# Seven more 1 MB weight buffers from spent storage, and more experts side by side in fours

## The reference, cut to what matters

```python
# first block: 32 experts, D_EXPERT = 256 (4 groups of 8: best group, then top 2 inside)
hid = silu(t @ w1[e]) * (t @ w3[e]);  out += gate[:, e] * (hid @ w2[e])
# second block: 16 experts, D_FF_EXPERT = 1024 (4 groups of 4: best group by its top-2 sum)
h = silu(t @ w_gate[e]) * (t @ w_up[e]);  y += gate[:, e] * (h @ w_down[e])
```

## Time and profile before

| what | us |
|---|---|
| median of 3 runs (lowest, highest) | 1676.85 (1676.71, 1677.9) |
| the profiled execution's own time | 1679.42 |
| its span, first to last instruction | 1676.2 |
| PE busy | 1570.4 (94%) |
| mean rate of DMA over the span | 241 GB/s, 404.40 MB |
| first mixture, first up matmul to last combine | about 727 to 962 |
| second mixture, the same | about 1189 to 1656 |

### The profile page before, as it was taken

The page is one execution under the profiler, slowest core; times in us unless marked ns, Lnnn a source line. Parts: engine busy times, 40 slices in busy tenths (PEclk is TensorE's granted clock), DMA queues, the critical chain, the costliest instruction groups (busy, mean ns, idle before and its releaser), DMA issues.

```text
span 1676.2 us, 21651 instructions
## 1 busy us (share of the span) xinstructions
PE 1570.4 (94%) x8351; PEld 1015.5 (61%) x8351; DVE 554.8 (33%) x1144; ACT 342.0 (20%) x731; POOL 148.8 (9%) x170
## 2 busy tenths in 40 slices
PE   6899999999999999999988999989999999999986
PEld 2577777677698888855544489658543544443433
DVE  2566767766522101262212110572501111101002
ACT  2344334344321100111100111441100000000001
POOL 1323442323200000000000000000000000000000
PEclk9999999999999999999999999999999999999999
DMA  9611111111944444549999974005499999999993
GB/s 374 252 39 46 42 44 43 38 38 50 373 151 136 145 151 151 199 169 389 421 421 421 421 268 151 25 1 181 194 422 421 421 408 421 421 422 400 422 421 140
DMA packets 58861, 404.40 MB, mean 241 GB/s; under 512 B 6766, under 2 KB 6898, under 8 KB 12576
## 3 DMA queue, kind: packets, MB, share of 16 engines
q1 hardware_dynamic: 52704, 381.92, 56.8%
q0 software_dynamic: 6080, 21.39, 4.3%
HBM read 402.19 MB, written 1.10 MB: 241 GB/s over the span
## 4 chain that ended last, share of the span: by engine, by line
PE 78%; DMA 9%; DVE 7%; issue 2%; ACT 2%; POOL 1%; SPq 1%; DVEq 0%; ACTq 0%; POOLq 0%
PE bank L656 76%; DMA ring<-in_moe 6%; DMA arena<-in_moe 2%; DVE arena L1728 2%; ACT arena L1370 1%; PE bank L1121 1%; POOL arena L600 1%; DMA xc<-in_xc 0%; DVE arena L1810 0%; ACT hc L1370 0%; DMA decay_rows<-arena 0%; DVE arena L1778 0%; DVE arena L1782 0%; DVE arena L1785 0%; DVE arena L1784 0%
## 5 line engine op out<-in xcount | busy, mean ns | idle before, releaser
L656 PE MATMUL bank<-arena 128*128 128x128 f32 (+3 forms) x3000 | 482.0, 311 | 28.6 <-DVE arena L1780 15.3
L656 PE MATMUL bank<-ring,arena 128*64 128x512 f32 (+2 forms) x1608 | 459.6, 604 | 25.3 <-DMA ring<-in_moe 18.1
L656 PEld LDWEIGHTS bank<-arena 128*128 128x128 f32 (+1 forms) x3000 | 394.3, 188 | 140.3 <-issue 50.3
L1370 ACT ACTIVATE arena<-bank 128x256 f32<-128x256 f32 (+2 forms) x372 | 161.2, 447 | 1112.7 <-PE bank L656 833.9
L656 PEld LDWEIGHTS bank<-ring,arena 128*64 128x64 f32 (+2 forms) x1608 | 144.1, 137 | 243.6 <-issue 239.1
L656 PE MATMUL bank<-hc,head_w 128*128 128x512 f32 (+1 forms) x384 | 162.5, 525 | 7.0 <-DVE arena L1802 6.6
L2130 DVE TENSOR_TENSOR arena<-arena,bank 128x256 f32<-128x256 f32 x48 | 20.2, 421 | 343.4 <-ACT arena L1370 343.4
L656 PE MATMUL bank<-arena,ring 128*128 128x256 f32 x416 | 92.3, 379 | 1.2 <-DVE arena L1907 1.2
L656 PE MATMUL bank<-hc,ring 128*128 128x256 f32 x416 | 91.4, 379 | 0.0
L656 PE MATMUL bank<-o_heads,arena 128*64 128x512 f32 (+2 forms) x184 | 85.3, 608 | 1.3 <-DMA ring<-in_moe 1.3
L656 PEld LDWEIGHTS bank<-arena,ring 128*128 128x128 f32 x416 | 79.0, 190 | 12.3 <-DVE arena L1907 1.6
(11 more groups left out here) (272 smaller groups left out, 1285.4 us busy)
## 6 DMA issues: line engine op xcount, KB each, us to landing
ring<-in_moe SPq DMA_DIRECT2D x201, 1024.0 KB, 17.3
ring<-in_dense SPq DMA_DIRECT2D x62, 1024.0 KB, 7.2
o_heads<-in_moe SPq DMA_DIRECT2D x23, 1024.0 KB, 18.1
xc<-in_moe SPq DMA_DIRECT2D x22, 1024.0 KB, 17.0
arena<-in_moe SPq DMA_DIRECT2D x21, 1024.0 KB, 19.4
hc<-in_moe SPq DMA_DIRECT2D x21, 1024.0 KB, 17.2
head_w<-in_head_w POOLq DMA_DIRECT2D x27, 512.0 KB, 3.9
xc<-in_dense SPq DMA_DIRECT2D x7, 1024.0 KB, 5.0
```

Of the source, the lines that this page charges most:

```text
L656: return nc.tensor.matmul(out, lhsT, rhs_, start=start, stop=stop, **kw)
L1370: return nc.scalar.activation(out, in_, func, **kw)
```

## The change

It turns seven more regions into homes for 1 MB loads. `ring` grows from 9 to 11, with storage from a smaller DMA scratch (`dynamic_dma_scratch_size=4096`) and from keeping the bias row of the spatial gating in the arena. Five spent regions join: `masks` (most of the constant matrices and ba_w, from load 37), `head_w` (from load 56, the first mixture's first), `normed` (H, once its rows are copied), `routing` and `places` (the routing's scratch, once the slots are spread). `head_w` is given back for the attention tables, of which POOL now loads only the routing's part (128 KB) at the old place and the rest once the load numbered 134 in `ORDER` has been used. The routing's small tiles move within the arena. In the first mixture ranks 6 to 9 become a fifth quad; in the second ranks 10 to 13 become a quad. So the units go from 12 to 11 and from 9 to 8, and the second mixture's steps from 36 to 32. The bytes of weights are the same. The ranking has four more small operations in the second mixture. The fallback `every_token` rebuilds H by transposes. The five warming matmuls read one matrix four times in place of four.

```diff
-RING = 9
+RING = 11
...
-SECOND_ORDER = [0, 3, 1, 4, 5, 2, 6, 7, 8]
-FIRST_ORDER = [0, 1, 2, 8, 3, 9, 4, 10, 5, 11, 6, 7]
+SECOND_ORDER = [0, 3, 1, 4, 7, 2, 5, 6]
+FIRST_ORDER = [0, 1, 2, 6, 3, 7, 8, 4, 9, 10, 5]
 PLACE = [FIRST_ORDER, SECOND_ORDER]
 FIXED = (6, 2)
-CUT = (10, 2)
+CUT = (6, 2)
+NARROW = (6, 10)
...
-    units += [("pair", ("ranked", r), ("ranked", r + 1)) for r in range(2, E2 - 2, 2)]
+    units += [("pair", ("ranked", r), ("ranked", r + 1)) for r in range(CUT[1], NARROW[1], 2)]
+    units += [("quad", *[("ranked", r + j) for j in range(4)]) for r in range(NARROW[1], E2 - FIXED[1], 4)]
...
+SHARED_SEMS = {RING - 2: ("vec_landed", 16), RING - 1: ("xc_landed", 16), "masks": ("mats_landed", 32),
+               "head_w": ("rel_set", 1), "normed": ("bias_copied", 2),
+               "routing": ("beta_made", 1), "places": ("g_ready", 1)}
...
     joins = {RING: ("x_ctx", "modulated", 1),
              G0 // BLOCKS: ("heads", "gdn_normed", 4),
-             first + RING + 2: ("tokens", "rest_taken", 5 * KT),
-             first + RING + 3: ("squares", "norm_summed", 1),
-             second + RING + 2: ("tokens", "out2_made", KT),
-             second + RING + 3: ("squares", "ln_var", 1)}
+             G0 // BLOCKS + 1: ("masks", "gdn_normed", 4),
+             first: ("head_w", "sgu_taken", KT),
+             first + RING + 4: ("tokens", "rest_taken", 5 * KT),
+             first + RING + 5: ("squares", "norm_summed", 1),
+             first + RING + 6: ("normed", "rows_copied", 4),
+             first + RING + 11: ("routing", "slots_spread", 1),
+             first + RING + 12: ("places", "slot_rows_made", 2),
+             second + RING + 4: ("head_w", "heads_squared", 8),
+             second + RING + 5: ("tokens", "out2_made", KT),
+             second + RING + 6: ("squares", "ln_var", 1),
+             second + RING + 11: ("routing", "order_ready", 2),
+             second + RING + 12: ("places", "slot_rows_made", 4)}
...
         if n == between:
-            free = [f for f in free if f[0] not in ("tokens", "squares")]
+            head_w_used = max(used for home, used in free if home == "head_w")
+            free = [f for f in free if f[0] not in ("head_w", "tokens", "squares", "routing", "places")]
...
                 if FREE_AT[n] > 0:
                     sp.wait_ge(slots_used, FREE_AT[n])
+                elif HOME[n] in SHARED_SEMS:
+                    sp.wait_ge(landed[HOME[n]], SHARED_SEMS[HOME[n]][1])
+                if HOME[n] == "places" and n in JOINS:
+                    sp.wait_ge(s["order_ready"], JOINS[n][2] // 2)
...
+            pool.wait_ge(s["head_free"], HEADS + 1)
+            pool.dma_start(sgu_row, t["rows"][:, 0:D]).then_inc(s["tables_landed"], 16)
             pool.wait_ge(s["residual"], 1)
             pool.dma_start(arena[:, 10752:10752 + KT * (GROUPS1 + E1 + E2)], t["router_w"]).then_inc(s["router_landed"], 16)
-            pool.dma_start(hw[:, 0:1024 + 4 * P], t["attn"]).then_inc(s["attn_landed"], 16)
+            pool.dma_start(hw[:, 0:2 * P], t["attn"][:, 0:2 * P]).then_inc(s["attn_landed"], 16)
+            pool.wait_ge(slots_used, HEAD_W_USED)
+            pool.dma_start(hw[:, 2 * P:4 * P + 1024], t["attn"][:, 2 * P:]).then_inc(s["attn_landed"], 16)
...
-                link(ts_(free_[:, 0:n], rank[:, 0:n], float(cut), None, ALU.min))
+                into = base[:, first:experts]
+                link(ts_(free_[:, 0:n], rank[:, 0:n], float(narrow), None, ALU.min))
                 link(tt_(free_[:, 0:n], free_[:, 0:n], rank[:, 0:n], ALU.add))
...
+                link(ts_(into, free_[:, 0:n], float(CAP // 2), CAP * first - FAR, ALU.mult, ALU.add))
+                if m == 1:
+                    link(ts_(free_[:, 0:n], rank[:, 0:n], float(cut), float(CAP), ALU.min, ALU.mult))
+                    link(tt_(into, into, free_[:, 0:n], ALU.add))
+                link(ts_(free_[:, 0:n], rank[:, 0:n], narrow - 0.5, float(CAP // 2), ALU.is_gt, ALU.mult))
+                link(tt_(counts_f[:, first:experts], kept_counts[:, first:experts], free_[:, 0:n], ALU.add))
...
-    nc = bacc.Bacc("TRN2", target_bir_lowering=False, num_devices=1)
+    nc = bacc.Bacc("TRN2", target_bir_lowering=False, num_devices=1, dynamic_dma_scratch_size=4096)
```

More of the change, by code:

```diff
@@ L167 @@
     ("g_heads", KT), ("slot", E1 // 2), ("dt_bias", DH), ("a_log", DH))
-MATS = ["ident", "tri_f", "tri_b", "same"] + [f"off{k}" for k in range(LEVELS)] + [f"pick{k}" for k in range(1, LEVELS)]
+MATS = ["ident", "same", "tri_f", "tri_b"] + [f"off{k}" for k in range(LEVELS)] + [f"pick{k}" for k in range(1, LEVELS)]
 def shape_constants():
@@ L189, in shape_constants @@
     d = (np.arange(P)[:, None, None] + P * np.arange(QT)[None, :, None]) - q[None, None, :]
-    attn = np.concatenate([before.reshape(P, -1), count(d).reshape(P, -1), after, s + t == P - 1, s < t, t + 0 * s], 1).astype(np.float32)
+    attn = np.concatenate([s < t, t + 0 * s, before.reshape(P, -1), count(d).reshape(P, -1), after, s + t == P - 1], 1).astype(np.float32)
     dist = SEQ - 1 - np.arange(BIAS_W)
@@ L383, in build @@
         base = area(12592, E1)
[L384 to L388, removed]
+        rank = area(16144, E1)
+        rank_t = area(16176, E1)
+        order_f = area(16208, E1)
+        order_u = area(12704, E1).bitcast(U32)
+        base_fixed = area(16240, E1)
         def pick(n):
-            return area(15744, n, n)
+            return area(15360, n, n)
         most = area(12688, 1).bitcast(U32)
@@ L406, in build @@
         attn_c = hw
[L407 to L412, removed]
+        earlier = attn_c[:, 0:P]
+        slot_numbers = attn_c[:, P:2 * P]
+        before = attn_c[:, 2 * P:2 * P + 512].rearrange("p (a n) -> p a n", a=QT)
+        count = attn_c[:, 2 * P + 512:2 * P + 1024].rearrange("p (a n) -> p a n", a=QT)
+        after = attn_c[:, 2 * P + 1024:3 * P + 1024]
+        flip = attn_c[:, 3 * P + 1024:4 * P + 1024]
         rel = o_heads[0:BUCKETS + 1, 0, 0:H2]
@@ L425, in build @@
         s = Sems()
-        landed = {home: sem(f"slot_{home}_landed") for home in (*range(RING), "x_ctx", "heads", "tokens", "squares")}
-        apart = {"x_ctx": XS, "heads": o_heads[:, :, :], "tokens": y_tokens, "squares": HS}
+        landed = {home: sem(f"slot_{home}_landed") for home in (*range(RING - 2), "x_ctx", "heads", "tokens", "squares")}
+        landed.update({home: s[name] for home, (name, _) in SHARED_SEMS.items()})
+        apart = {"x_ctx": flat(XS), "heads": flat(o_heads[:, :, :]), "tokens": flat(y_tokens), "squares": flat(HS),
+                 "normed": flat(H), "masks": first_w[:, 2 * P:2 * P + GROUP], "head_w": hw[:, 2 * P:2 * P + GROUP],
+                 "routing": area(10240, GROUP), "places": area(14336, GROUP)}
         def slot_at(n):
             home = HOME[n]
-            return apart[home].rearrange("p a b -> p (a b)") if home in apart else ring[:, home, :]
+            return apart[home] if home in apart else ring[:, home, :]
         slots_used = sem("slots_used")
@@ L1196, in every_token @@
                 src = H if m == 0 else X
+                if m == 0:
+                    for k in range(KT):
+                        for qt in range(QT):
+                            at = (k % 2) * SEQ + qt * P
+                            ins = nc.tensor.transpose(bank[4 + k // 2][:, at:at + P], own_rows[:, qt, k * P:(k + 1) * P], M("ident"))
+                    ins.then_inc(s["all0_pe"], 1)
+                    pe.wait_ge(s["all0_act"], 4)
+                base_pe, base_act = ((1, 4), (0, 0))[m]
                 pe.sem_inc(s[f"all{m}_used"], 1)
@@ L1596, in every_token @@
                 experts, sub = (E1, E2)[m], SUBS[m]
+                base_pe = (1, 0)[m]
+                if m == 0:
+                    act.wait_ge(s["all0_pe"], 1)
+                    for i in range(4):
+                        act_fn(flat(H[:, 2 * i:2 * i + 2, :]), bank[4 + i][:, :], ACT.Copy).then_inc(s["all0_act"], 1)
                 with act.Fori(0, experts) as e:
@@ L1940, in rank_experts @@
             def rank_experts(m, kept_counts):
-                experts, first, cut = (E1, E2)[m], FIXED[m], CUT[m]
+                experts, first, cut, narrow = (E1, E2)[m], FIXED[m], CUT[m], NARROW[m]
                 n = experts - first
@@ L2205, in every_token @@
                                     ALU.mult, ALU.add).then_inc(own, 1)
-                dve.wait_ge(s[f"all{m}_pe"], 6 * sub * experts + 1)
+                dve.wait_ge(s[f"all{m}_pe"], base_pe + 6 * sub * experts + 1)
             mixture(0, *route1())
```

58 lines of the change are left out of this document (28 added, 30 removed).

## The result

The changed kernel takes 1647.87 us by the median of 4 runs (1645.95 to 1650.18), against 1677.14 (1676.71 to 1677.9, 4 runs) for the kernel before on the same chip: a ratio of 0.9826, 95% interval 0.9809 to 0.9843. The profiled execution took 1646.8 us, with a span of 1645.1 against 1676.2. The forecast was 1650 (1641 to 1662), faster.

The account below looks back on a forecast made before the run. The weight stream was taken to bound both mixtures. Gains of 11.5 us in the first and 15.0 in the second, 26.5 together, off the median of 1676.85 gave 1650.4, range 1641 to 1662.

Parts of the forecast that it names:

- The bound: Both mixtures end when the stream of weights ends, at 421 GB/s or 2.49 us a load, not with PE.
- The start of the first mixture: 16 loads stand ready; load 16 waits for the experts' order, is issued at 733.0 and lands at 737.7.
- The first mixture's gain: First mixture: last combine 12.8 us earlier, at 945.5; 11.5 us after the clock's charge; bounds 1 to 16.
- charge for the clock: First mixture's tail after a quad: a lower clock may double 3.65 us of matmul; 1.3 charged.
- The tables: First mixture: 0.66 MB of attention tables now fall into its weight stream, costing 1.6 us.
- The second mixture: Second mixture: five loads less to wait for (12.4 us) plus 2.6 of idle time, 15.0; bounds 12.4 to 19.5.
- the stream's own idle time: Second mixture: 7.1 us lost before; 4.5 kept for stalls that aren't full homes, citing the 396 GB/s window.
- The quads: Both mixtures: five quads and one new quad cost no PE time on the path; units saved gain 0.
- The stream didn't slow: Rival, chance 0.06: more outstanding loads or new homes lower the stream's rate; at 396 GB/s, 1689 us.
- No home came too late: Rival, chance 0.04: a late join stops all loads behind it on SP; time stays near 1676 us.
- The first mixture did give its share: Rival, chance 0.17: first mixture gains little (1 us), held by order, tables and quads at the tail; 1661 us.
- All of it counts: Rival, chance 0.12: lost time goes completely in both mixtures, 16 + 19.5 = 35.5 us, so 1641.

Follow-up runs that it names:

- homes alone: The changed kernel with all seven new homes but the units of the kernel before (12 and 9): 1653.05 us, ratio 0.9839.
- quads only: The changed kernel with its new units (11 and 8) but the 13 homes of before: 1676.54 us, ratio 0.9988.
- two fewer homes: The changed kernel without the two new homes of ring, so 18 homes: 1655.21 us, ratio 0.9858.
- eight fixed experts: The changed kernel with eight fixed experts in place of six in the first mixture: 1651.1 us in one run.
- the changed kernel once more: The changed kernel, unedited, run again on another set's chip for comparison: 1649.19 us, ratio 0.983.
- attention's filler: 1.7 us of unread matmuls in attention's first head: 1649.81 us added to the changed kernel, 1645.77 added to the one with eight fixed experts and late tables.
- tables late: The changed kernel with the 640 KB of attention tables loaded once the first mixture's output is normed: 1647.86 us in one run.
- parent: The changed kernel with eight fixed experts and late attention tables, no added matmuls: 1645.56 us (ratio 0.9809) in one set, 1649.31 (0.9822) in another.
- both fillers: The parent plus unread matmuls in attention (1.7 us) and ahead of the first mixture's last quad's down (6.8 us): 1646.3 us, ratio 0.9814.

## Why the prediction was right

**The bound.** Right: homes alone gave 25 us, quads alone about 2, and quads only kept its 333 and 413 GB/s.

**The start of the first mixture.** Right: the first ranked load was issued at 732.48 (forecast 733.0) and landed at 737.5 (737.7). That the order and not storage bounds what stands ready is shown by two fewer homes (M1 unchanged) and by eight fixed experts (M1 2.1 less).

**The first mixture's gain.** The load that was to land at 933.1 ended PE's wait at 932.98, and the last combine was to start at 945.5 ahead of the charge for the clock; it starts at 945.61. The charge of 1.3 wasn't paid in this profile. It was 1.7 in the changed kernel once more and 2.9 in the one with attention's filler, a mean of 1.5 over the three. So 1.3 is fair as a mean, and that this profile paid nothing is luck. The Trainium skill ("TensorE: Matmul & The Clock Gate", What's actually happening) has the idle state as the throttled one; by that the full charge falls due when PE has been idle long enough. The rows agree in direction and not in size: nothing behind 2.18 us of idle time, 2.9 of the full 3.65 behind 4.99.

**The tables** were charged 1.6; tables late measures 1.3.

**The second mixture.** 15.0 forecast, 17.1 measured. The five loads that stand ready were right: two homes less cost 5.1, as 2 x 2.49 says. The term that was mis-sized is the stream's own idle time, kept at 4.5 of 7.1. The changed kernel has 173 intervals from 1183.5 to 1616.5, 433.0 us, against 430.8 at full rate: 2.2 lost. The window of 396 GB/s was read as a stall that homes don't cure; in the changed kernel no slice of the second mixture is below 421 save the first and the last.

**The quads** were put at 0 both ways. Alone they are, nearly. On top of the homes they are worth 2.9 us in the second mixture, because the homes make PE the bound there. The forecast named that limit, but as a case that the change avoids, and didn't say that part of its 26.5 hangs on the quads.

**Between the mixtures** nothing was forecast and 1.6 us came. Before runs 3.4 us at the lower clock in attention's first head (from 1062.8) and the changed kernel does not; that this is the whole of it is argued, not shown. The changed kernel once more has 234.0, so a part may be chance.

**The sum**: 26.5 forecast, 31.1 of span and 29.3 by the medians. Off are M2 (2.1 more), between (1.6) and the first mixture's end (1.2, the clock's charge), and 0.3 the other way behind the last combine. M2's part comes back in every profile. The other two are luck of this execution: the changed kernel once more has a span of 1647.9.

**The rivals.** The stream didn't slow: 421 and 422 GB/s with more loads outstanding, where the Trainium skill ("HBM Reference", Specifications (TRN2)) has about 425 for a core alone; the rows agree. No home came too late: 16 and 18 loads stood ready, and load 18 was the first to be issued in the second mixture. The first mixture did give its share. "All of it counts" was the nearest rival: the second mixture came within 2.4 of its 19.5.

## What to carry to other kernels

A buffer more is worth one whole transfer's time where it stands full when the stretch begins (two that joined later gave 3.0 us together here, in place of 5); find first what lets the first transfer go (here the order of experts in one mixture, storage in the other). Faster compute pays almost nothing while the stream is the bound, and more buffers stop paying once compute is, so price them together: what one saves is hidden until the other has moved. When runs of one kernel fall into two groups, look for a stretch whose code is the same and whose duration isn't.

## What the runs showed of the hardware that was not expected

**SP's issues are held back when many loads are outstanding.** In the changed kernel 10% of the chain that ended last is SP's queue at line 508, in pieces like the 889.09 row above, 1.99 us; the earlier trace rows has 0.33 for a single issue. All issues of one home, and the time from issue to landing:
```profile
L508 SPq DMA_DIRECT2D ring<-in_moe x163: 327/333/6128, 608.6 to 1590.3; - x163
```
```profile
DMA to landing us min/median/max: 4.7/23.8/32.4
```
The median from issue to landing rose from 17.3 to 23.8 us and its maximum from 27.9 to 32.4, some 13 loads of 2.49; an issue to this home then takes up to 6.1 us. Counted from issue and landing of every weight load after 600 us, an issue takes 0.33 to 0.41 us by the mean while at most nine others are outstanding, 1.86 with ten and 2.82 with eleven. The rate is 421 GB/s in nearly all slices of both mixtures, so the loads wait at SP in place of in the queue, and no rate was lost. It would cost if something urgent stood behind them on SP's queue.

**The lower clock comes to different places of the same code.** In attention a low stretch of 13.7 us costs 6 us of *between*, and it was there in four profiles of the eleven without a filler. With 1.4 and 0.8 us of idle time covered by matmuls it is absent in three profiles of three, and by their times none of ten runs of the faster kernel had it, where four of the parent's ten did. But the changed kernel has the same idle time (1.43 and 0.78 us) and no low clock behind it, so idle time is not the whole condition; what else decides stays open. The version with eight fixed experts, late tables and attention's filler has no run above 1646.35: 1645.77 us, 31.5 below the kernel before beside it. By ratio (0.981) it isn't told from its parent's better set (0.9809) or from the one with both fillers (0.9814).
